# Gate products from a rounded gate and its rest, and 80 fetch steps in the gate stage

## What is computed

```python
e = jnp.take_along_axis(cidx, pos, axis=-1)
g = jax.nn.softmax(top, axis=-1)
act = jax.nn.gelu(jnp.einsum('thkd,td->thk', u_tab[e], xb), approximate=False)
w = (g * act).astype(xb.dtype)
return jnp.einsum('thk,thkd->td', w, v_tab[e])
```

## Time and profile before

| | |
|---|---|
| median of 3 runs | 4101.98 us (4083.38 to 4104.35) |
| profiled execution | 4086.75 us, its span 4085.0 us |
| PE busy in the span | 3619.7 us (89%) |
| DVE busy | 2974.4 us (73%) |
| ACT busy | 1466.7 us (36%) |
| gate stage, first and second layer | about 1090 to 1488 and 3140 to 3540 us |
| values stage, first and second layer | about 1492 to 2020 and 3544 to 4070 us |

### The profile page before, as it was taken

The page is one execution under the profiler, slowest core; times in us unless marked ns, Lnnn a source line. Parts: engine busy times, 40 slices in busy tenths (PEclk is TensorE's granted clock), DMA queues, the critical chain, the costliest instruction groups (busy, mean ns, idle before and its releaser), DMA issues. The chain is left out here.

```text
span 4085.0 us, 53350 instructions
## 1 busy us (share of the span) xinstructions
PE 3619.7 (89%) x19146; PEld 3148.0 (77%) x19146; DVE 2974.4 (73%) x6542; ACT 1466.7 (36%) x2418; POOL 607.9 (15%) x523
## 2 busy tenths in 40 slices
PE   7655777989999989999888887888899999899999
PEld 5523556789999988888766664666899999888887
DVE  3564354389899988888767575243798999888887
ACT  3412333333333333333344453323333334333332
POOL 0000000000144432222100000000001444322221
PEclk9877889999999999999999998898999999999999
DMA  3071121345699999999521201213355999999996
GB/s 125 1 272 44 62 83 42 103 136 169 203 362 366 368 332 350 349 351 349 217 91 56 73 14 44 77 55 103 122 164 194 354 372 368 332 345 354 350 352 247
DMA packets 371206, 853.00 MB, mean 209 GB/s; under 512 B 35952, under 2 KB 185072, under 8 KB 368880
## 3 DMA queue, kind: packets, MB, share of 16 engines
q1 hardware_dynamic: 256624, 529.59, 37.5%
q0 software_dynamic: 73728, 268.47, 17.8%
q10 hardware_dynamic: 40592, 51.53, 3.6%
HBM read 753.91 MB, written 94.37 MB: 208 GB/s over the span
## 5 line engine op out<-in xcount | busy, mean ns | idle before, releaser
L912 POOL DMA_INDIRECT p2f_row<-in_expert_u_rows,p2f_index x128 | 158.7, 1240 | 1442.1 <-POOLq L82 1152.9
L912 POOL DMA_INDIRECT p1f_row<-in_peer_u_rows,p1f_index x128 | 158.5, 1238 | 1061.5 <-POOLq L82 771.5
L1494 PE MATMUL p2v_out<-p2a_u_hi,p2v_w_hi 128*128 128x512 f32 x768 | 299.8, 390 | 11.2 <-DVE p2v_w_lo L1476 11.2
L1494 PE MATMUL p1v_out<-p1a_u_hi,p1v_w_hi 128*128 128x512 f32 x768 | 299.9, 390 | 10.6 <-DVE p1v_w_lo L1476 10.6
L1494 PE MATMUL p1v_out<-p1a_u_lo,p1v_w_hi 128*128 128x512 f32 x768 | 299.6, 390 | 0.0
L1494 PE MATMUL p2v_out<-p2a_u_lo,p2v_w_hi 128*128 128x512 f32 x768 | 299.6, 390 | 0.0
L1494 PE MATMUL p1v_out<-p1a_u_hi,p1v_w_lo 128*128 128x512 f32 x768 | 299.5, 390 | 0.0
L1494 PE MATMUL p2v_out<-p2a_u_hi,p2v_w_lo 128*128 128x512 f32 x768 | 299.5, 390 | 0.0
L1454 ACT CAST p2a_u_hi<-p2a_u 128x1024 fp32r<-128x1024 f32 x128 | 135.0, 1055 | 328.4 <-PE p2v_out L1494 320.7
L1454 ACT CAST p1a_u_hi<-p1a_u 128x1024 fp32r<-128x1024 f32 x128 | 135.0, 1055 | 328.0 <-PE p1v_out L1494 321.0
L1473 DVE TENSOR_TENSOR p1a_u_lo<-p1a_u,p1a_u_hi 128x1024 fp32r<-128x1024 f32 x128 | 156.8, 1225 | 81.0 <-ACT p1a_u_hi L1454 72.0
(11 more groups left out here) (673 smaller groups left out, 10316.4 us busy)
## 6 DMA issues: line engine op xcount, KB each, us to landing
p1a_u<-in_peer_u SPq DMA_DIRECT2D x128, 512.0 KB
p1a_u<-in_peer_v SPq DMA_DIRECT2D x128, 512.0 KB
p2a_u<-in_expert_u SPq DMA_DIRECT2D x128, 512.0 KB
p2a_u<-in_expert_v SPq DMA_DIRECT2D x128, 512.0 KB
gates<-p_kept SPq DMA_DIRECT2D x20, 2048.0 KB
ad_w<-in_w_ada SPq DMA_DIRECT2D x12, 2048.0 KB
acts<-p1a_a ACTq DMA_DIRECT2D x128, 192.0 KB
p1w_a<-acts SPq DMA_DIRECT2D x128, 192.0 KB
```

The source lines that it names most:

```text
L912: self.nc.gpsimd.indirect_dma_start(self.row[:, n % self.RING, :], None, self.u_rows if dot else self.v_rows, bass.IndirectOffsetOnAxis(ap ...
L1494: last = nc.tensor.matmul(out[:, o, :], lhs[:, s, t * P:(t + 1) * P], rhs[:, n % VSLABS, cols], start=(n == 0 and m == 0), stop=(n == KEYS ...
```

## The change

In the gate stage, the gate row that goes into `hot1` is now the gate rounded to float32r, and `hot1` and `hot2` are float32r tiles. A second matrix holds the rest: ScalarE multiplies each token's `hot1` by gate_rest, which is (gate - rounded gate) / rounded gate, made once per layer by VectorE in five operations of 384 columns. TensorE multiplies hot2 by both in float32r and adds them in PSUM: two products for a token in the place of one f32 product. Every step now has one more semaphore, `rest_ready`, between ScalarE and TensorE. The new matrices lie in columns 0 to 127 of x_hi and x_lo, which `multiply` doesn't read, and the small rows in the second half of the buffer for stored gates; so the load of the second group of gates now waits until all 96 steps have their rest. And FETCHED_IN_GATES is 80, not 128.

```diff
-FETCHED_IN_GATES = 128
+FETCHED_IN_GATES = 80
...
+        hot1, hot2 = (sb(n, [P, RING, TOK, KEYS], F32R) for n in ("hot1", "hot2"))
+        hot1_rest = [x[:, TOK * n:TOK * (n + 1), 0:P] for x in (A.x_hi, A.x_lo) for n in range(2)]
...
+            dve.wait_ge(top_made, 1)
+            ch.add(V.tensor_copy(gate_top, gate_hi))
+            ch.add(V.tensor_scalar(floor, gate_hi, TINY, None, ALU.max))
+            ch.add(V.tensor_tensor(gate_rest, gate[:], gate_hi, ALU.subtract))
+            ch.wait()
+            ch.add(V.reciprocal(floor, floor))
+            ch.wait()
+            V.tensor_tensor(gate_rest, gate_rest, floor, ALU.mult).then_inc(rest_known, 1)
...
                             nc.vector.tensor_scalar(hot1[:, r, q, :], C["iota"][:, 0:KEYS], first[:, token:token + 1],
-                                                    gate[:, token:token + 1], ALU.is_equal, ALU.mult)
+                                                    gate_top[:, token:token + 1], ALU.is_equal, ALU.mult)
...
                         pe.wait_ge(hot_ready, s + 1)
+                        pe.wait_ge(rest_ready, s + 1)
...
                         for q in range(TOK):
-                            last = nc.tensor.matmul(prod[:, r, q, :], hot2[:, r, q, :], hot1[:, r, q, :],
-                                                    start=True, stop=True, skip_group_check=True)
+                            for m, hot in enumerate((hot1[:, r], hot1_rest[r])):
+                                last = nc.tensor.matmul(prod[:, r, q, :], hot2[:, r, q, :], hot[:, q, :],
+                                                        start=(m == 0), stop=(m == 1), skip_group_check=True)
...
+            act.wait_ge(hot_ready, s + 1)
+            for q in range(TOK):
+                token = s * TOK + q
+                last = nc.scalar.mul(hot1_rest[r][:, q, :], hot1[:, r, q, :], gate_rest[:, token:token + 1])
+            last.then_inc(rest_ready, 1)
...
+                    for q in steps_after(i):
+                        rest_of_hot(act, t * STEPS + q)
                     A.gelu(act, base + t * LATE + i)
...
-            for group in range(2):
-                W.load_gates(sp, group)
+            W.load_gates(sp, 0)
+            sp.wait_ge(rest_ready, PIECES * STEPS)
+            W.load_gates(sp, 1)
```

More of the change, by code:

```diff
@@ L20 @@
 EPS = 1e-6
+TINY = 1e-30
 MASKED = -1e30
@@ L1312, in peer_gates @@
         sb, ps, sem = phase_tools(nc, ctx, tag)
-        hot1 = sb("hot1", [P, RING, TOK, KEYS])
-        hot2 = sb("hot2", [P, RING, TOK, KEYS])
+        hot1, hot2 = (sb(n, [P, RING, TOK, KEYS], F32R) for n in ("hot1", "hot2"))
+        hot1_rest = [x[:, TOK * n:TOK * (n + 1), 0:P] for x in (A.x_hi, A.x_lo) for n in range(2)]
+        gate_hi = hot1[:, 0].rearrange("p q k -> p (q k)")[:, 0:DENSE]
+        spare = W.g[:, 1].rearrange("p a g t -> p (a g t)")
+        gate_rest, floor, gate_top = (spare[:, n * DENSE:(n + 1) * DENSE] for n in range(3))
         prod = ps("prod", [P, RING, TOK, KEYS])
@@ L1317, in peer_gates @@
         hot_ready, hot_free, prod_free = sem("hot_ready"), sem("hot_free"), sem("prod_free")
+        step, top_made, rest_known, rest_ready = (sem(n) for n in ("step", "top_made", "rest_known", "rest_ready"))
         stored = [sem(f"stored{s}") for s in range(KEPT_PIECES)]
@@ L1323, in steps_after, with rest_of_gates @@
             return range(STEPS * i // LATE, STEPS * (i + 1) // LATE)
+        def rest_of_gates(dve):
+            V = nc.vector
+            ch = Chain(dve, step)
+            dve.wait_ge(top_made, 1)
[6 more added lines that the diff above has]
+            V.tensor_tensor(gate_rest, gate_rest, floor, ALU.mult).then_inc(rest_known, 1)
         @block.vector
@@ L1329, in _ @@
                     A.split_lo(dve, base + t * LATE + i)
+                    if t == 0 and i == 0:
+                        rest_of_gates(dve)
                     for s in (t * STEPS + q for q in steps_after(i)):
@@ L1360, in _, with rest_of_hot @@
                         for q in range(TOK):
-                            last = nc.tensor.matmul(prod[:, r, q, :], hot2[:, r, q, :], hot1[:, r, q, :],
-                                                    start=True, stop=True, skip_group_check=True)
+                            for m, hot in enumerate((hot1[:, r], hot1_rest[r])):
+                                last = nc.tensor.matmul(prod[:, r, q, :], hot2[:, r, q, :], hot[:, q, :],
+                                                        start=(m == 0), stop=(m == 1), skip_group_check=True)
                         last.then_inc(hot_free, 1)
+        def rest_of_hot(act, s):
+            r = s % RING
+            act.wait_ge(hot_ready, s + 1)
[3 more added lines that the diff above has]
+            last.then_inc(rest_ready, 1)
         @block.scalar
         def _(act):
+            nc.scalar.copy(gate_hi, gate[:]).then_inc(top_made, 1)
+            act.wait_ge(rest_known, 1)
             for t in range(PIECES):
                 for i in range(LATE):
+                    for q in steps_after(i):
+                        rest_of_hot(act, t * STEPS + q)
                     A.gelu(act, base + t * LATE + i)
```

## The result

| | before | changed |
|---|---|---|
| median | 4097.55 us (12 runs, 4083.1 to 4104.35) | 4076.05 us (12 runs, 4060.11 to 4083.73) |
| ratio | | 0.9945, 95% interval 0.9932 to 0.9958 |
| span of the profiled execution | 4085.0 us | 4062.2 us |

The kernel became faster by 0.55%, where 4152 us and 1.2% slower was forecast. All executions counted here are fast ones; of the kernel before's runs beside the last four experiments one was slow, at 7425 us, and the ratios leave it out.

The account below looks back on a forecast made before the run. The prediction took TensorE, VectorE and DMA engines as limits in the gate stage, TensorE alone in the values stage. A layer: 0 plus +25 us; two layers +50 on 4102 give 4152 us, range 4084 to 4206.

Parts of the forecast that it names:

- So the DMA engines become the bound: Values stage: 48 more fetches make 200.0 MB, 379 GB/s in 528 us, more than the DMA engines give; +25 us a layer.
- No stretch of this trace comes near it: Values stage: reason for setting aside the skill's 425 GB/s, by which the stage would hide the 379 GB/s asked for.
- The transfers are hidden: Rival: values stage takes the 48 fetches behind TensorE, gate stage moves up to 4 us; 4094 to 4112 us, chance 0.20.
- Of its 11.0 us of idle time I give it back 4: Gate stage: TensorE, alone at its limit after the change, regains 4 us of its idle time.
- The 4 us put against it: Gate stage: TensorE's first product waits once for VectorE's and ScalarE's preparation of the rests; 4 us, making the stage's sum 0.
- the last two slices are empty: Values stage's end: last transfers land some 14 us before it, added on top unless the tail shrinks; 547 to 561 us.
- The products themselves: Gate stage: float32r products at 0.111 us each, 768 making 85 us, cost what the old did; -2 to +7 us a layer.
- 0.067 us of the moving columns: Rival on gate-stage products: 768 take 51 us, 34 less; 4084 us, or 4034 with transfers hidden; chance 0.12.
- the doubled one: Rival: each narrow float32r product costs an f32 product's two records, 0.222 us; gate stage +85 us a layer, 4320 us, chance 0.08.
- ScalarE's new place holds TensorE up: Rival in the gate stage: +12 us a layer or more on top of the forecast, 4176 us; chance 0.15.
- now it holds up the products of the next tile: Gate stage: a late u tile, before covered by two tiles, delays the next tile's products; put at 0, upper end +12 a layer.
- The lower DMA load is what shortens these waits: Gate stage: fewer transfers cut ScalarE's waits for u tiles, 101 us before, to well below that.

Follow-up runs that it names:

- the last four experiments: Four follow-up kernels measured as one group on one chip, beside 15 runs of the kernel before with median 4098.19 us.
- half_48: Kernel before with 48 fetch steps in the gate stage and half of the columns in VectorE's sums of the values stage; 4127.54 us, ratio 1.0066.
- half_24: Kernel before with 24 fetch steps in the gate stage, VectorE taking half of the columns in steps 24 to 151; 4213.14 us, ratio 1.0279.
- half_sums: Kernel before, VectorE multiplying and adding only 512 of 1024 columns of the 128 rows taken in the gate stage; 4069.13 us, ratio 0.9914.
- move_alone: Kernel before with FETCHED_IN_GATES = 80 and nothing else, products still single f32 ones; 4056.79 us, ratio 0.9877.
- half_rows: Kernel before, 96 of the gate stage's 132 fetches bringing only the rows of tokens 0 to 63; 4100.27 us, ratio 0.9991.

## Why the prediction was wrong

**The step that failed is "So the DMA engines become the bound".** The term of +25 us a layer for the values stage (its working gave +19 to +33) measured 0.1. Its amounts were right: 200.0 MB and 379 GB/s forecast, 199.56 MB and 380 in the window. Its mechanism exists too, as half_48 and half_24 show. Wrong was the limit that it was held against. I took 372 GB/s, the best slice of 102 us, and the 358 of a stage with a share of 1.00. Both show what was asked for, not what can be had: the limit is 405, and no slice of the values stage before stood at it. The rows that said so stood there: single slices of 392, which I noted and kept for the lower end alone. The gate stage of the same trace said it more clearly. Its mean of 358 is made of slices of 10 us between 263 and 416:

```profile
GB/s 313 263 332 291 332 384 387 325 375 416 343 369 410 334 347 356 380 366 381 411 276 376 406 346 366 396 368 335 385 405 354 385 405 305 371 407 357 310 323 347
```

Seven of the 40 are at 405 or above. So "No stretch of this trace comes near it" was false for stretches of 10 us, and the stage was not at a limit of 358: half_sums moved 371 in it.

The busy share misled in the same way. The middle of the values stage, 1510 to 1990 us, in the kernel before:

```profile
1510.00:1990.00 480.00, 480.00 (x2120) 397.58 (x2119) 405.44 (x643) 173.16 (x239) 118.87 (x121) 1.00 0.96 350
```

And in the changed one:

```profile
1510.00:1990.00 480.00, 480.00 (x2120) 397.63 (x2119) 456.60 (x714) 180.03 (x241) 219.06 (x166) 1.00 1.03 401
```

A share of 0.96 at 350 GB/s had room for 15% more. My sum of busy times, 480 + 67 = 547 us, took packet times as fixed, and the changed kernel has 0.98 x 525 = 515 us. Part of this is that packets got shorter: in the values stage the software queue took 0.330 x 16 x 528 us / 17902 = 0.156 us a packet before and 0.442 x 16 x 525 / 24768 = 0.150 in the changed kernel. The Trainium skill ("DMA: Bandwidth & Descriptors", Bandwidth), whose 425 GB/s I set aside for these rows, was nearer: half_48 holds 404, which is 5% below it and 9% above my 372. By the same section of the Trainium skill each core gets about 358 GB/s when both cores of a pair stream; this program runs on one core, and no run here shows that case.

**The first rival, "The transfers are hidden", is what happened in the values stage.** It got 0.20. Even so its time, 4100, would have been 24 too high, by the gate stage and the gap.

**The gate stage** was forecast at 0 and gave 7.4 us. "Of its 11.0 us of idle time I give it back 4" was too little: in move_alone the stage is 10.1 us shorter, the pauses gone and the granted clock at 1.00 instead of 0.99. The 4 us put against it were for the wait of the first product, and there only 1.6 us lie between it and multiply's last. That the products cost 3 to 5 us in all at 80 steps is near the 4 by luck.

**The gap** was not in the forecast. I had given each stage its own sum and treated the barrier as nothing; it was worth 6.6 us a layer, nearly half of the gain, by GpSimd's drain.

**The tail** of the values stage was misread: "the last two slices are empty" holds for the last one alone, and the one before has 110 GB/s. By these the last transfer lands some 22 us before 2020 and not 14. The term fell for another reason, so this changed nothing.

**The products themselves** were right. They start 0.111 us apart, the time that 128 columns of weights took to load in the earlier trace rows:

```profile
1244.74 0.27 PE L1383 MATMUL p1g_prod<-p_x_lo,p1g_hot 128*128 128x128 f32 x1
1244.85 0.27 PE L1383 MATMUL p1g_prod<-p1g_hot 128*128 128x128 f32 x1
1244.96 0.28 PE L1383 MATMUL p1g_prod<-p_x_lo,p1g_hot 128*128 128x128 f32 x1
```

So both rivals on their pace fell, the 0.067 us of the moving columns and the doubled one, and the 81 ns at 128 columns of the Trainium skill ("TensorE: Matmul & The Clock Gate", Back-to-back issue gap) do not hold for these. Other amounts: VectorE 338.22 us in the gate stage (334 forecast), ScalarE 259.26 (147.6 + 111 = 258.6), VectorE 491.67 in the values stage (496), the 384 one-hot rows 107.4 us with a float32r result and 106.8 before. The later load of the second group of gates kept nobody waiting.

**"ScalarE's new place holds TensorE up"** described the mechanism word for word ("now it holds up the products of the next tile"), and with 128 steps it is there, 27 us a layer in the gate stage. At 80 steps it costs almost nothing, but "The lower DMA load is what shortens these waits" gave half of the reason at most. With the old products fewer transfers shortened them not at all (111.5 us in half_rows against 101.0), and less work on VectorE did (49.4); with the new ones each took off about a third (32.1 and 33.7 us against 48.8).

With the measured terms the sum would have been -7.4 - 6.6 + 0.1 a layer, 4102 - 28 = 4074 us.

For the kernel this means: the products gave nothing, since two float32r products of 0.111 us cost what the two records of an f32 product did, and 80 steps gave everything. The kernel before with 80 steps is at least as fast as the changed one. By the limit of 405 GB/s a tile of 4.09 us can bring 1.66 MB, of which 0.885 are v, activations and gates; that leaves 1.48 fetches a tile, 183 in the stage. As an estimate from these numbers, the values stage begins to grow below about 73 steps in the gate stage; no run stands between 80 and 48.

## What to carry to other kernels

- A rate that a profile shows is what was asked for until somebody waits. Before a stage is called full, look for engines that wait for transfers and for slices that stand flat at one value; a busy share near 1.00 is neither. Look at fine slices as well as long ones: those of 10 us in the gate stage before had 416 GB/s, those of 102 us at most 372. If the forecast hangs on the limit, the range must hold both sides of it.
- When an engine is relieved, look at all that its signals start: here VectorE's lead let ScalarE's wait for u tiles shrink from 101.0 to 10.8 us, and GpSimd's drain end before TensorE's last product.
- An added wait of the bounding engine is priced by what stands ahead of the releasing instruction in its queue. With 128 steps the rests cost 27 us a layer behind a wait for a tile and 4 ahead of it.

## What the runs showed of the hardware

- With the loads of the values stage one core moved 404 GB/s over 480 us at a stretch (half_48), with a share of 1.03. Single slices of 10 us in the gate stage, where stores run too, reached 416 (before). Below that the share says little: 0.96 at 350 GB/s; and in the gate stage 1.00 at 358, 0.97 at 295, 0.91 at 306, 1.01 at 371.
- GpSimd's drain at the barrier ended 6.9 to 11.9 us after its last indirect DMA was issued, over both layers of all traces (1484.44 to 1495.10 before, 1477.83 to 1487.20 in the changed kernel), and 0.7 to 4.9 us after the last packet of these had landed. A barrier behind a later end of the drain waited for it.
- A pause of TensorE of 8.8 us was followed by products of 384 columns 0.32 us apart instead of 0.17, with a granted clock of 0.50, which is 1.2 in place of 2.4 GHz. The two windows of 52 us with that pause and the one of 5.0 us behind it had a granted clock of 0.90 and 0.93.
